# Column sums in place of dummy products between the two blocks of a two-block model

## The reference, cut to what matters

```python
def first_block(x, ...):
    h = x
    for l in range(DEPTH):
        ...
        h = h + conv_ffn(rmsnorm(h, ffn_norm[l]), w_up[l], conv_w[l], conv_b[l], w_down[l])
    return rmsnorm(h, final_norm)

def rms_norm(x, g):
    xf = x.astype(jnp.float32)
    y = xf * lax.rsqrt(jnp.mean(xf * xf, axis=-1, keepdims=True) + EPS)
    return (y * g.astype(jnp.float32)).astype(x.dtype)

def modulate(h, shift, scale):
    return h * (1.0 + scale[:, None, :]) + shift[:, None, :]
```

## Time and profile before

| | us |
|---|---|
| median of 3 runs | 1786.39 (1786.35 to 1786.55) |
| the profiled execution, its own time | 1786.81 |
| its span, first to last instruction | 1785.1 |
| TensorE busy | 1755.8 (98%) |
| VectorE, ScalarE, GpSimd busy | 1116.6, 779.5, 1037.8 |

### The profile page before, as it was taken

The page is one execution under the profiler, slowest core; times in us unless marked ns, Lnnn a source line. Parts: engine busy times, 40 slices in busy tenths (PEclk is TensorE's granted clock), DMA queues, the critical chain, the costliest instruction groups (busy, mean ns, idle before and its releaser), DMA issues. The chain is left out here.

```text
span 1785.1 us, 25898 instructions
## 1 busy us (share of the span) xinstructions
PE 1755.8 (98%) x8977; PEld 1434.9 (80%) x8977; DVE 1116.6 (63%) x1827; ACT 779.5 (44%) x1271; POOL 1037.8 (58%) x1264
## 2 busy tenths in 40 slices
PE   8999999999999999999999999999999999999998
PEld 6877888888888887788888888878666878999996
DVE  4787666666656337766666665554486567666665
ACT  5445443333334335453333333457576663333332
POOL 6584555565465658265465565447411568888885
PEclk9999999999999999999999999999999999999999
DMA  7221223443423221133443332412301112233221
GB/s 257 95 104 51 96 90 134 153 158 114 151 94 119 95 97 57 48 107 117 142 164 131 132 125 94 142 49 96 118 1 48 48 48 95 95 109 118 106 95 47
DMA packets 103206, 184.70 MB, mean 103 GB/s; under 512 B 7322, under 2 KB 67404, under 8 KB 101068
## 3 DMA queue, kind: packets, MB, share of 16 engines
q1 hardware_dynamic: 102940, 183.44, 29.3%
q10 hardware_dynamic: 176, 0.07, 0.0%
HBM read 180.35 MB, written 2.10 MB: 102 GB/s over the span
## 5 line engine op out<-in xcount | busy, mean ns | idle before, releaser
L1003 POOL TENSOR_TENSOR w_lo<-raw,w_hi 128x256 fp32r<-128x256 f32 (+1 forms) x1124 | 912.9, 846 | 728.5 <-ACT w_hi L1087 722.2
L1087 ACT ACTIVATE w_hi<-raw 128x1024 fp32r<-128x1024 f32 (+2 forms) x331 | 307.6, 937 | 358.6 <-PE ps L2537 231.4
L2524 PE MATMUL ps<-n_hi,w_hi 128*128 128x512 f32 (+1 forms) x1120 | 429.0, 385 | 0.0
L2525 PE MATMUL ps<-n_lo,w_hi 128*128 128x512 f32 (+1 forms) x1120 | 426.6, 383 | 0.0
L2530 PE MATMUL ps<-n_hi,w_lo 128*128 128x512 f32 (+1 forms) x1120 | 272.9, 383 | 0.0
L2524 PEld LDWEIGHTS ps<-n_hi,w_hi 128*128 128x128 f32 x1120 | 209.8, 187 | 43.4 <-issue 2.2
L2525 PEld LDWEIGHTS ps<-n_lo,w_hi 128*128 128x128 f32 x1120 | 210.1, 188 | 40.9 <-issue 0.2
L2530 PEld LDWEIGHTS ps<-n_hi,w_lo 128*128 128x128 f32 x1120 | 206.1, 187 | 41.6
L2050 DVE TENSOR_TENSOR ps<-ps,sq 128x512 f32<-128x512 f32 x88 | 61.3, 699 | 178.2 <-PE ps L2530 175.9
L1300 ACT ACTIVATE zc<-ps,cpar 128x512 f32<-128x512 f32 x88 | 68.3, 776 | 196.3 <-DVE ps L2050 196.3
L2071 DVE TENSOR_TENSOR h<-h,ps 128x512 f32<-128x512 f32 x176 | 111.3, 679 | 64.6 <-PE ps L2537 62.7
(11 more groups left out here) (402 smaller groups left out, 3242.6 us busy)
## 6 DMA issues: line engine op xcount, KB each, us to landing
raw<-in_w_up SPq DMA_DIRECT2D x44, 1024.0 KB, 7.0
raw<-in_w_ff SPq DMA_DIRECT2D x32, 1024.0 KB, 6.1
raw<-in_w_in SPq DMA_DIRECT2D x26, 1024.0 KB, 6.2
zb<-in_ada_w SPq DMA_DIRECT2D x16, 1536.0 KB, 8.4
raw<-in_w_down SPq DMA_DIRECT2D x44, 512.0 KB, 4.0
raw<-in_w_out SPq DMA_DIRECT2D x12, 1024.0 KB, 5.9
raw<-in_w_in SPq DMA_DIRECT2D x4, 512.0 KB, 8.2
za<-in_x SPq DMA_DIRECT2D x4, 512.0 KB, 6.0
```

The lines of the kernel that those rows point to most:

```text
L1003: last = pool.tensor_tensor(part[0], part[1], part[2], ALU.subtract)
L1087: act.activation(split_quarter(st.kind, w_hi, g % 4, q), source(st, q), ACT.Copy).then_inc(whi_ready, 1)
L2524: pe.matmul(out, pairs[0][0], pairs[0][1], start=start and k == ks[0], stop=False)
L2525: pe.matmul(out, pairs[1][0], pairs[1][1], start=False, stop=False)
```

## The change

Seven dummy products go: those of the first two gaps. In the first gap stand three column sums in their place, in the second six. The loop behind the spread keeps its dummies and its sums, but sums other tiles. Nine sums are left for the groups `k = 1` to `7`, where eighteen were. The numbers of tiles that `beside_first` sums are 1, 1, 1, 2, 1, 1, 2 now; they were 2, 3, 2, 3, 2, 3, 3. The sums and their results are the same.

```diff
             final_sums((DT - 2,))
-            streamed(2)
+            modulation_sums(1, range(0, 3))
             final_sums((DT - 1,))
-            streamed(5)
+            modulation_sums(1, range(3, 9))
             spread(("mix2",), NT, ("final",))
-            for t in range(6):
+            for t in range(9, 15):
                 streamed(1)
                 modulation_sums(1, range(t, t + 1))
             streamed(1)
...
-                    modulation_sums(1, range(6 + 18 * (k - 1) // 7, 6 + 18 * k // 7))
+                    modulation_sums(1, range(15 + 9 * (k - 1) // 7, 15 + 9 * k // 7))
```

## The result

The changed kernel takes 1788.78 us (median of 22 runs, 1785.51 to 1790.38), the kernel before 1786.05 (22 runs, 1784.51 to 1788.57): a ratio of 1.0012 [1.0007, 1.0018]. That is 2.1 us more (0.0012 x 1786.05; by the interval 1.3 to 3.2): clear of zero, and less than the 0.2% (3.6 us) that the prediction took as its bound. The profiled execution took 1788.70 us, its span is 1787.0.

What follows compares the result with a forecast made beforehand. TensorE's own queue, busy for 98% of the span, was taken to bound the kernel. First product +2.2, first six products +1.2, nine saved sums -1.8 gave +1.6 us: 1788.4 profiled, 1788.0 as a median, range 1784.4 to 1790.0.

Steps and rivals of the forecast that it cites:

- (B): Between the blocks, clock low through the loop, back once the first six products have run: +1.6 us, 1788.0; chance 0.36.
- (A): Between the blocks, clock falls but returns at 1151.90 as before, within the loop: -1.6 us, 1784.8; chance 0.17.
- (C): Between the blocks, the clock does not fall at all: -3.2 us, 1783.2; chance 0.05.
- (F): Whole kernel: no effect, the shift is absorbed further on, 1786.4 us; chance 0.05.
- (E): Low clock outlasts the first products: +3.0 us with one further group, +4.4 (1790.8) with two; chance 0.12.
- First gap: Three sums for two dummies: last eight norm sums start within 0.1 us of before; cost 0 to 0.1, taken as 0.05.
- Second gap: Six sums for five dummies: clock falls at 1148.48 as before, transposes 0.33 us later, at 1149.82.
- Loop and first products: Behind the transposes: low-clock turns of 0.85, first product 2.2 us later, first six products 1.2 us more.
- Later groups: Nine of 18 sums leave the groups at 0.20 us each: 1.8 us less, groups of 1.64 with one sum.
- Sum at the place: Between the blocks and in the groups behind: +2.2 + 1.2 - 1.8 = +1.6 us.
- (D): (B) plus a second clock fall ahead of the last feed-forward, product there 1.4 us later: +3.0, 1789.4; chance 0.25.
- The page's rule: Clock drops after idle gaps between matmul bursts; the changed queue has none, so by it the clock stays up, (C).

Runs made afterwards that it cites:

- experiment 1: The kernel before with the seven dummies of the first two gaps taken out and nothing in their place: 1788.89 us, ratio 1.0015 against before.
- experiment 5: The kernel before with the second gap's five dummies replaced by six sums, the first gap's two dummies kept: 1789.34 us, ratio 1.0013 against before.
- experiment 8: The changed kernel with 15 dummies added in TensorE's waits ahead of the second block's feed-forward: 1788.08 us, ratio 1.0007 against before.
- experiment 3: The changed kernel with the loop's seven dummies taken out too, its six sums kept: 1786.79 us, ratio 1.0001 against before.
- Experiment 4: The kernel before with the first gap's two dummies replaced by three sums, the second gap's five dummies kept: 1786.16 us, ratio 0.9999 against before.
- experiment 2: The kernel before with all dummies kept and nine column sums of the groups not computed at all: 1784.48 us, ratio 0.9992 against before.

## Why the prediction was right, by its steps

**The forecast.** 1788.0 was foretold and 1788.78 measured, at the upper edge of the likeliest case's own 1787.4 to 1788.8. The chain of causes of (B) is what the runs show: the wide products leave the second gap (experiments 1 and 5), the clock is low through the loop (turns of 0.86), and comes back while the first six products run (1157.80, and 1158.80 in experiment 8). (A) and (C), by which it would have been faster, fall: all five traces without the wide products of the second gap have a fall, and none a return after 3.4 us. That is said of the usual execution: three of the change's 22 runs took 1785.5 to 1785.9, and none of the profiles is of such a run. (F) falls with the ratio's interval. (E) wasn't seen: in each of the five traces the clock was back by the first product of the second group, or (experiment 3) 0.1 us into it.

**First gap.** Cost 0 to 0.1: the last norm sums start 1148.10 - 1146.60 = 1.50 behind the zero, before 1.40: +0.10. Experiment 4 agrees, with a time that isn't told from before's.

**Second gap.** The sum took the fall where before had it, 3.0 behind the zero. In the profiled execution it came at 4.4, so the transposes came 0.29 sooner, which is the text's figure for the full clock (0.27). In experiment 8 it came at 2.7, and the transposes 0.63 later, where 0.33 was the figure. So when the clock falls is no constant of the kernel, and the prediction took it for one.

**Loop and first products.** +2.2 foretold for the first product: +1.06 here, +2.53 in experiment 8 (11.09 against 8.56), by when the fall came. The six products: 1158.33 - 1156.22 = 2.11 up to the second spread of `rstd` against 1.38, so +0.73 (+0.87 in experiment 8), and 1.2 foretold: the clock was back in their midst, not behind them. This term was too large. The text's reading that TensorE's own queue sets the first product holds only where the clock has fallen: in the four traces without a fall between the blocks it comes 7.26 behind the zero, whatever stands in the gaps, and just behind the `n_lo` that it waits for (in experiment 2 ready at 1151.45 + 1.24 = 1152.69, product at 1152.83).

**Later groups.** A sum at 0.20 and nine at 1.8: measured 0.22 and 2.0. Groups of one sum at 1.64: 1.62.

**Sum at the place.** +1.6 foretold against before's profile; -0.21 in one execution of the changed place and +1.38 in another. What the text didn't weigh is that before's profile is one draw as well: it had a fall worth 24.00 - 22.79 = 1.2 us. The price of the change at the place is a mean over executions on both sides, which no pair of profiles gives. That the total fits so well is therefore partly luck: the terms move by more than the sum missed, and in the profiled pair the loss lies at 724 and at the second place.

**The second place.** (D) was given 0.25, and is what the profiled execution did: the twenty passes and four more at the low level, 1.30 us where 1.4 was foretold. Whether it belongs to most executions of the change stays open: in the kernels of experiments 5 and 2 a fall of 3.4 us lies there and costs nothing (6.69 and 6.68), and experiment 8 leaves its share of the 2.1 us open. (B) and (D) are therefore not told apart as the typical case, only both from the rest. The fall at 724 wasn't thought of.

**The page's rule.** By the Trainium skill, "TensorE: Matmul & The Clock Gate", section "Why this matters for your kernels", long idle gaps between bursts of matmuls are what costs the clock in the middle of a kernel. Neither trace has a gap as long as the section means: the longest hole in experiment 1 is 1.19 us, and the change was busy for 3.88 of 3.97 us before its fall. The clock fell in both, so the rule is not enough here, and the measurement decides: without such a gap the clock can fall too.

## What to carry to other kernels

A dummy product in a wait can be worth its place though it computes nothing: here real work in its stead would have gained only if it had kept the clock as well, and the columns of short passes did not, though TensorE was almost always busy. Read the granted clock of a stretch beside its busy share, and where the clock falls in some executions only, judge by the times of many runs, with the mean clock beside them, since a pair of profiles compares two draws. Where the clock has already fallen, each dummy ahead of the first real product costs its double time (0.41 in experiment 3), so cover that doesn't hold the clock should go.

## What was not expected of the hardware

The clock falls in parts that no edit touched: 724.31 to 727.72 in the changed kernel (and at 725.16 in experiment 5), in the middle of other work, at a price of 1.4 us each time, and in the profile of before nowhere near. Runs of one kernel differ by 4 us (1784.6 to 1789.2 for before), and the mean granted clock, between 0.996 and 1.000, goes with it. The low stretches inside the kernels last 3.4, 6.8 or 10.2 us in these rows. Their price between the blocks, by the ends with the same number of sums: 1.2 us for 3.4 (24.00 against 22.79), 3.0 for 6.8 (23.79 against 20.78), 4.4 to 4.6 for 10.2 (26.01 against 21.65, 25.38 against 20.78).
